# Scalar-tensor-tensor forms on VectorE and a later turn of the probabilities in a two-block transformer forward pass

## What is computed

```python
logits = jnp.einsum('bqhd,bkhd->bhqk', qf[:, q0:q1], kf[:, :q1]) * scale
bias = c[:, :, q0:q1, None] - c[:, :, None, :q1]
logits = jnp.where(mask[None, None], logits + bias, NEG)
p = jax.nn.softmax(logits, axis=-1)
outs.append(jnp.einsum('bhqk,bkhd->bqhd', p, vf[:, :q1]))
```

```python
acc = conv_b
for j in range(CONV_W):
    acc = acc + a_pad[:, j:j + L] * conv_w[j]
return jnp.einsum('blf,fd->bld', jax.nn.silu(acc) * b, w_down)
```

## Time and profile before

| | |
|---|---|
| median of three runs | 2684.56 us |
| the profiled execution | 2669.68 us, its span 2667.7 us |
| TensorE matmuls busy | 2459.9 us (92%), 12039 matmuls |
| GpSimd, ScalarE, VectorE busy | 1205.8, 897.2, 866.2 us |
| chain that ended last | TensorE 75%, GpSimd 9%, issue 8%, VectorE 4%, ScalarE 3% |
| granted TensorE clock, mean | 0.96 |

### The profile page before, as it was taken

The page is one execution under the profiler, slowest core; times in us unless marked ns, Lnnn a source line. Parts: engine busy times, 40 slices in busy tenths (PEclk is TensorE's granted clock), DMA queues, the critical chain, the costliest instruction groups (busy, mean ns, idle before and its releaser), DMA issues.

```text
span 2667.7 us, 31984 instructions
## 1 busy us (share of the span) xinstructions
PE 2459.9 (92%) x12039; PEld 1981.4 (74%) x12039; DVE 866.2 (32%) x1466; ACT 897.2 (34%) x1247; POOL 1205.8 (45%) x1032
## 2 busy tenths in 40 slices
PE   7898989979999989888888999998899989999997
PEld 6676757657888867766776888886688778889886
DVE  2434343441122131356543111222445322313222
ACT  3223232243322343344434332234432223323222
POOL 4353444434444446566553444444521234555552
PEclk8898989789999999999999999999999999999999
DMA  3211212112222212211112222321311111332331
GB/s 104 64 47 63 61 49 63 48 47 95 95 94 94 94 55 87 56 47 39 47 48 72 95 93 91 98 94 48 91 48 48 47 49 48 95 94 79 94 88 55
DMA packets 230943, 188.56 MB, mean 71 GB/s; under 512 B 8960, under 2 KB 222397, under 8 KB 230733
## 3 DMA queue, kind: packets, MB, share of 16 engines
q1 hardware_dynamic: 227152, 183.66, 22.4%
q10 hardware_dynamic: 3708, 3.79, 0.5%
HBM read 185.30 MB, written 2.10 MB: 70 GB/s over the span
## 4 chain that ended last, share of the span: by engine, by line
PE 75%; POOL 9%; issue 8%; DVE 4%; ACT 3%; DMA 0%; SPq 0%; POOLq 0%; DVEq 0%; ACTq 0%
PE ps L2232 54%; PE ps L1219 7%; POOL w_lo L1610 5%; PE ps L587 2%; PE ps L2263 1%; PE ps L2376 1%; PE ps L2354 1%; PE ps L1278 1%; PE ps L1189 1%; PE ps L1327 1%; POOL a_lo L1618 1%; PE ps L2379 1%; POOL xs L1665 1%; ACT w_hi L1737 1%; PE ps L1323 0%
## 5 line engine op out<-in xcount | busy, mean ns | idle before, releaser
L1610 POOL TENSOR_TENSOR w_lo<-raw,w_hi 128x512 fp32r<-128x512 f32 (+2 forms) x728 | 892.6, 1257 | 1013.6 <-ACT w_hi L1737 1013.4
L2232 PE MATMUL ps<-a_hi,w_hi 128*128 128x512 f32 (+1 forms) x1744 | 637.6, 382 | 61.7 <-POOL w_lo L1610 24.3
L2232 PE MATMUL ps<-a_lo,w_hi 128*128 128x512 f32 (+1 forms) x1744 | 629.7, 378 | 0.0
L2232 PE MATMUL ps<-a_hi,w_lo 128*128 128x512 f32 (+1 forms) x1744 | 629.7, 377 | 0.0
L1737 ACT ACTIVATE w_hi<-raw 128x2048 fp32r<-128x2048 f32 (+2 forms) x182 | 328.3, 1804 | 508.1 <-PE ps L2232 446.2
L2232 PEld LDWEIGHTS ps<-a_hi,w_hi 128*128 128x128 f32 x1744 | 323.0, 191 | 145.0 <-issue 64.9
L2232 PEld LDWEIGHTS ps<-a_hi,w_lo 128*128 128x128 f32 x1744 | 322.9, 192 | 62.2 <-issue 1.0
L2232 PEld LDWEIGHTS ps<-a_lo,w_hi 128*128 128x128 f32 x1744 | 322.1, 192 | 62.9
L2232 PE MATMUL ps<-b_hi,w_hi 128*128 128x512 f32 x912 | 360.2, 395 | 7.5 <-POOL b_lo L1678 4.3
L2232 PE MATMUL ps<-b_hi,w_lo 128*128 128x512 f32 x912 | 361.3, 396 | 0.0
L2232 PE MATMUL ps<-b_lo,w_hi 128*128 128x512 f32 x912 | 359.4, 394 | 0.0
(11 more groups left out here) (302 smaller groups left out, 2810.2 us busy)
## 6 DMA issues: line engine op xcount, KB each, us to landing
raw<-in_mlp_w_dram SPq DMA_DIRECT2D x128, 512.0 KB, 4.3
raw<-in_w_up_dram SPq DMA_DIRECT2D x44, 512.0 KB, 5.0
raw<-in_ssd_w_in_dram SPq DMA_DIRECT2D x32, 512.0 KB, 4.7
raw<-in_hgrn_w_in_dram SPq DMA_DIRECT2D x24, 512.0 KB, 4.6
raw<-in_w_in_dram SPq DMA_DIRECT2D x24, 512.0 KB, 4.9
raw<-in_ssd_w_out_dram SPq DMA_DIRECT2D x16, 512.0 KB, 4.5
raw<-in_ple_w_gate_dram SPq DMA_DIRECT2D x16, 512.0 KB, 4.0
raw<-in_w_down_dram SPq DMA_DIRECT2D x16, 512.0 KB, 4.0
```

Of the source, the lines that this page charges most:

```text
L1610: last = nc.gpsimd.tensor_tensor(w_lo[:, slot, piece], raw[:, slot, piece], w_hi[:, slot, piece].bitcast(F32), ALU.subtract)
L2232: last = nc.tensor.matmul(ps[:, b + s, 0:nn], w[:, k, m * P:(m + 1) * P], v[:, k, c0 + s * nn:c0 + (s + 1) * nn], start=(k == 0 and first) ...
```

## The change

All edits but two turn a VectorE instruction into a scalar_tensor_tensor that computes the same: `(in0 * 1.0) op in1` instead of `in0 op in1`. In L1042 a per-row scalar product becomes a product with the scalar and with a column of ones read with stride 0; in L1152 scale and bias by two per-row scalars becomes a scale by a scalar and a sum with the bias column read with stride 0. The low parts of the weights are made in four pieces in both kernels. In TensorE's attention steps with keys beyond the meta tokens (qb above 0) the fills are cut in two, with the values between, and the turn of the next step comes behind all of them.

```diff
@@ hgrn_dve, level
-  nc.vector.tensor_tensor(halves_of(hdd[:, i % 4], m, True), up, ref, ALU.subtract)
+  nc.vector.scalar_tensor_tensor(out=halves_of(hdd[:, i % 4], m, True), in0=up, scalar=1.0, in1=ref,
+                                 op0=ALU.mult, op1=ALU.subtract)
-  nc.vector.tensor_tensor(halves_of(hdd[:, i % 4], m, False), ref, low, ALU.subtract)
+  nc.vector.scalar_tensor_tensor(out=halves_of(hdd[:, i % 4], m, False), in0=ref, scalar=1.0, in1=low,
+                                 op0=ALU.mult, op1=ALU.subtract)
@@ hgrn_dve, end of a head; alike: roped (add), gated of retention (mult), summed (add),
@@ mlp_dve's b_lo (subtract), ple_dve's addition (add), the SSD groups' em by cbm (mult)
-  nc.vector.tensor_tensor(ho[:].unsqueeze(1), ho[:].unsqueeze(1), xc[:, bass.ds(h, 1), 0:T], ALU.mult)
+  nc.vector.scalar_tensor_tensor(out=ho[:].unsqueeze(1), in0=ho[:].unsqueeze(1), scalar=1.0,
+                                 in1=xc[:, bass.ds(h, 1), 0:T], op0=ALU.mult, op1=ALU.mult)
@@ block2_dve, normed
-  nc.vector.tensor_scalar(fp[0:q, n % 2, 0:nk], fp[0:q, n % 2, 0:nk], fm[0:q, n % 2, 3:4], None, ALU.mult)
+  nc.vector.scalar_tensor_tensor(out=fp[0:q, n % 2, 0:nk], in0=fp[0:q, n % 2, 0:nk],
+                                 scalar=fm[0:q, n % 2, 3:4], in1=ones[0:q, 0:1].broadcast_to([q, nk]),
+                                 op0=ALU.mult, op1=ALU.mult)
@@ block2_dve, ffn
-  own.did(nc.vector.tensor_scalar(acc[:], au[:, 4:516], taps[2], taps[3], ALU.mult, ALU.add))
+  own.did(nc.vector.scalar_tensor_tensor(out=acc[:], in0=au[:, 4:516], scalar=taps[2],
+                                         in1=taps[3].broadcast_to([P, T]), op0=ALU.mult, op1=ALU.add))
@@ block2_pe, the attention steps
-                fill(per_step[s] if n < N_FOX - 2 else 3)
+                half = per_step[s] // 2 if n < N_FOX - 2 else 1
+                if qb:
+                    fill(half)
+                    values(n)
+                    fill((per_step[s] if n < N_FOX - 2 else 3) - half)
+                else:
+                    fill(per_step[s] if n < N_FOX - 2 else 3)
                 if n + 1 < N_FOX:
                     turn_p(n + 1)
-                if qb:
-                    values(n)
```

More of the change, by code:

```diff
@@ L508, in level @@
                     ref = low[:, :, m - 1:m].broadcast_to([P, T // (2 * m), m])
-                    nc.vector.tensor_tensor(halves_of(hdd[:, i % 4], m, True), up, ref,
-                                            ALU.subtract).then_inc(dd_ready, 1)
+                    nc.vector.scalar_tensor_tensor(out=halves_of(hdd[:, i % 4], m, True), in0=up, scalar=1.0, in1=ref,
+                                                   op0=ALU.mult, op1=ALU.subtract).then_inc(dd_ready, 1)
                     if before:
                         dve.wait_ge(*before)
-                    nc.vector.tensor_tensor(halves_of(hdd[:, i % 4], m, False), ref, low,
-                                            ALU.subtract).then_inc(dd_ready, 1)
+                    nc.vector.scalar_tensor_tensor(out=halves_of(hdd[:, i % 4], m, False), in0=ref, scalar=1.0, in1=low,
+                                                   op0=ALU.mult, op1=ALU.subtract).then_inc(dd_ready, 1)
                 def scores(i):
@@ L552, in head @@
                 dve.wait_ge(on_ready, h * 2 + 1)
-                nc.vector.tensor_tensor(ho[:].unsqueeze(1), ho[:].unsqueeze(1), xc[:, bass.ds(h, 1), 0:T],
-                                        ALU.mult).then_inc(on_ready, 1)
+                nc.vector.scalar_tensor_tensor(out=ho[:].unsqueeze(1), in0=ho[:].unsqueeze(1), scalar=1.0,
+                                               in1=xc[:, bass.ds(h, 1), 0:T], op0=ALU.mult,
+                                               op1=ALU.mult).then_inc(on_ready, 1)
                 b_at.add()
@@ L1041, in normed @@
                 own.wait()
-                nc.vector.tensor_scalar(fp[0:q, n % 2, 0:nk], fp[0:q, n % 2, 0:nk], fm[0:q, n % 2, 3:4], None,
-                                        ALU.mult).then_inc(f_pn, 1)
+                nc.vector.scalar_tensor_tensor(out=fp[0:q, n % 2, 0:nk], in0=fp[0:q, n % 2, 0:nk],
+                                               scalar=fm[0:q, n % 2, 3:4], in1=ones[0:q, 0:1].broadcast_to([q, nk]),
+                                               op0=ALU.mult, op1=ALU.mult).then_inc(f_pn, 1)
             def by_sin(i, e):
@@ L1055, in roped @@
                     dve.wait_ge(r_sin, 2 * i + (e + 1))
-                    nc.vector.tensor_tensor(t, t, fv[e][:], ALU.add).then_inc(r_rope, 1)
+                    nc.vector.scalar_tensor_tensor(out=t, in0=t, scalar=1.0, in1=fv[e][:], op0=ALU.mult,
+                                                   op1=ALU.add).then_inc(r_rope, 1)
             def decayed(i, e, kb):
@@ L1081, in gated @@
                     dve.wait_ge(r_on, 2 * h + 1)
-                    nc.vector.tensor_tensor(ro[e][:], ro[e][:], gates[:, h, :], ALU.mult).then_inc(r_on, 1)
+                    nc.vector.scalar_tensor_tensor(out=ro[e][:], in0=ro[e][:], scalar=1.0, in1=gates[:, h, :],
+                                                   op0=ALU.mult, op1=ALU.mult).then_inc(r_on, 1)
                 b_at.add(2)
@@ L1974, in summed @@
                         own.wait()
-                    ins = nc.vector.tensor_tensor(lv[:, 0:T], res[:, 0, 0:T] if m == 1 else lv[:, 0:T], res[:, m, 0:T],
-                                                  ALU.add)
+                    ins = nc.vector.scalar_tensor_tensor(out=lv[:, 0:T], in0=res[:, 0, 0:T] if m == 1 else lv[:, 0:T],
+                                                         scalar=1.0, in1=res[:, m, 0:T], op0=ALU.mult, op1=ALU.add)
                     if m < KD - 1:
@@ L2018, in mlp_dve @@
                         dve.wait_ge(bhi_ready, b_at(1))
-                        nc.vector.tensor_tensor(b_lo[:, k, 0:T], hv[:, k % 4], b_hi[:, k, 0:T].bitcast(F32),
-                                                ALU.subtract).then_inc(blo_ready, 1)
+                        nc.vector.scalar_tensor_tensor(out=b_lo[:, k, 0:T], in0=hv[:, k % 4], scalar=1.0,
+                                                       in1=b_hi[:, k, 0:T].bitcast(F32), op0=ALU.mult,
+                                                       op1=ALU.subtract).then_inc(blo_ready, 1)
                         b_at.add()
@@ L2038, in ple_dve @@
                         dve.wait_ge(free_dve, fd(-1 if m < KD else 0))
-                        nc.vector.tensor_tensor(xc[:, m - 1, 0:T], xc[:, m - 1, 0:T], res[:, m - 1, 0:T],
-                                                ALU.add).then_inc(xc_ready, 1)
+                        nc.vector.scalar_tensor_tensor(out=xc[:, m - 1, 0:T], in0=xc[:, m - 1, 0:T], scalar=1.0,
+                                                       in1=res[:, m - 1, 0:T], op0=ALU.mult,
+                                                       op1=ALU.add).then_inc(xc_ready, 1)
                 pub.add(KD)
@@ L2148, in group @@
                     dve.wait_ge(em_ready, g * 8 + (r + 1))
-                    nc.vector.tensor_tensor(em[r % 3], em[r % 3], cbm[:].rearrange("p c l -> p (c l)"),
-                                            ALU.mult).then_inc(m_ready, 1)
+                    nc.vector.scalar_tensor_tensor(out=em[r % 3], in0=em[r % 3], scalar=1.0,
+                                                   in1=cbm[:].rearrange("p c l -> p (c l)"), op0=ALU.mult,
+                                                   op1=ALU.mult).then_inc(m_ready, 1)
                     if r + 2 < HPG:
```

## The result

The changed kernel takes 2694.52 us (median of 20 runs, 2683.02 to 2704.09) and the kernel before, run beside it, 2685.64 (20 runs, 2676.18 to 2691.91): a ratio of 1.0034, with an interval of 1.0020 to 1.0048, or +8.9 us. The forecast was +6 and 2690.5. The sum was nearly right, and the trace shows that it was right for a reason only partly the forecast one.

A forecast was written before the change was run, and what follows sets the result against it. TensorE was taken to bound the attention steps wholly. The terms 0 + 0 + 0 + 5.9 = +6 us made 2669.7 into 2675.6 on the profiled execution, 2690.5 us on the median, with a range of 2674 to 2703.

The forecast's parts named there:

- What bounds the kernel: TensorE bounds the attention steps wholly, busy 154.23 of 155.00 us; edits elsewhere pay only where TensorE waits.
- Part 1: VectorE's tensor_tensor turned into scalar_tensor_tensor with a constant scalar: taken as 0, between -0.7 and +3.5 us.
- 0.5 us a head: Sign against the forecast: an HGRN head shorter or longer by over 0.5 us.
- the faster rival: Forms free GpSimd or shorten VectorE's waits, shrinking HGRN and weight waits: -13 us, 2671; chance 0.15.
- Part 2: First tap of the gated MLP (L1152) loses its fast form: +0.27 us each, covered, cost 0.
- Part 3: Normalisation of attention probabilities (L1042) loses its fast form: 5.6 us of VectorE, cost 0 to +2 us, taken 0.
- Part 4: TensorE's new attention order: values stall for copies out of PSUM in seven steps, 5.9 us in sum.
- a slice 0.78: In attention, the fill slice between logits and values takes 0.78 us, counted towards the values' arrival at 1968.7.
- Sum: Whole kernel: 0 + 0 + 0 + 5.9 = +6 us, 2675.6 on the profiled execution, 2690.5 on the median.
- the stalls reach further: In attention, longer normalisation delays turn, copies and values in a chain: +16 us, 2700; chance 0.20.
- Halved throughput: New forms take +0.53 us per 512 columns in HGRN, mask products, norms and MLP: +48, 2732; chance 0.05.
- nothing: Attention order changes nothing, since ScalarE takes the copy before the weight chunk: 2684.6; chance 0.05.

The follow-up runs named there:

- e1: All scalar_tensor_tensor forms of the change, with TensorE's order as in the kernel before; 2687.05 us, ratio 1.0009.
- e2: TensorE's new order alone, with the VectorE forms of the kernel before; 2695.52 us, ratio 1.0039.
- e3: Kernel before, but a step's values come behind its whole fill and ahead of the next step's turn; 2684.1 us, ratio 0.9995.
- e5: Kernel before, but in 23 of 40 attention steps the previous step's values stand behind the first fill slice; 2702.46 us, ratio 1.0063.
- e6: Kernel before, but in 26 of 40 attention steps the logits stand behind the first fill slice; 2685.99 us, ratio 1.0019.
- e8: Change's order with the forms of before, but in steps s = 0, 3 and 6 values stand behind the whole fill; 2686.75 us, ratio 1.0017.
- e12: Kernel before, with the change's order in steps s = 3 to 7 alone (16 of 32 steps cut); 2689.0 us, one run.
- a tidy experiment: Change's order with the forms of before, but in steps s = 6 values come behind the whole fill; 2689.41 us, ratio 1.0013.
- e11: Kernel before, with the change's order in steps s = 6 and 7 alone (8 of 32 steps cut); 2688.05 us, ratio 0.9999.
- e13: The changed kernel profiled a second time, nothing altered; 2693.76 us, one run.

## Why the prediction was right, and where not

- **What bounds the kernel**: right. Only attention's length changed beyond the spread of executions; e1 and e2 show that the order alone makes the slowdown.
- **Part 1, constant-scalar forms at nothing**: right. 694 ns for 694, the level differences 418 for 418 (median), the product of decay and scores 684 for 684; the heads of HGRN begin 12.6 and end 13.6 us later than before, so all eight together are 1 us longer, under the 0.5 us a head that would have refuted it. GpSimd was not freed: the waits for the products of the levels are 24.0 us for 21.3, and that is no cost of the forms either, since they are 22.7 to 25.2 us in the runs with before's forms there (e2, e3, e5, e6, e8 to e12); the faster rival fell.
- **Part 2, first tap**: right in size and in cover. The last tile of a gated MLP round, after, with TensorE's wait for it; it answers to the earlier trace rows:

```profile
2369.65 1.09 DVE L1156 SCALAR_TENSOR_TENSOR acc<-au,pcol 128x512 f32<-128x512 f32 x1 [5.80 <-ACT au L938]
2370.89 1.56 DVE L1159 SCALAR_TENSOR_TENSOR acc<-au,pcol,acc 128x512 f32<-128x512 f32 x1
...
2374.52 0.69 DVE L1168 TENSOR_TENSOR hv<-acc,ps 128x512 f32<-128x512 f32 x1 [1.18 <-PE ps L2244]
```
```profile
PE ps L2244 <- DVE hv L1168: 3.0, 3, 1.0
```

  0.27 us longer (1.09 for 0.82), VectorE's idle time ahead of the product 0.27 shorter (1.18 for 1.45), TensorE's three waits unchanged.
- **Part 3, normalisation**: 0.77 us for 528 columns as worked out. Taken at 0 of 0 to 2: in before's order it costs two waits, 0.4 us, in the new order none.
- **Part 4, the new order**: the sum was right (5.9 forecast; 6.2 - 0.7 = 5.5 came), the list of waits was not. Behind n = 0, 13, 20 and 33 the wait for ScalarE's copy came as said, with 0.36, 0.70, 0.36 and 0.70 us for 0.8, 0.85, 0.8 and 0.85. Behind n = 6, 16 and 26, where 1.0, 0.6 and 1.0 stood, the values did not wait; the slice ahead of them did, 1.10, 1.02 and 1.10 us, for the bank under evacuation. Behind n = 36, where nothing stood, 0.3 us came by the same cause. The step that failed is "a slice 0.78", taken as work that can always start: I asked when the values' own inputs are ready, but not whether the slice that moves forward with them has its bank. The waits on ScalarE were put 1.2 us too high (3.3 for 2.1), the others 0.9 too low (2.6 for 3.5); that these nearly cancel is luck.
- **What was costed at nothing**: cutting the run of fill matmuls. It costs 0.1 us a time in 32 steps, 3.3 us in all, and moving the values ahead of the turn some 0.2. This is the term that is missing in "Sum". With it the account against the second profile nearly closes, in hundredths: 164.03 - 153.37 = 10.66 us = 5.56 waits + 3.32 first pairs + 0.25 place + 0.93 values of step 38 inside the stretch, and 0.60 not accounted for. Without the 0.93 the order costs 9.7 us in the trace, for 8.9 (whole change) and 10.6 (e2) in the timed medians.
- **The rivals**: the turn never waited for the normalisation in the changed kernel, against "the stalls reach further" (e5 shows that it can: seven such waits). Halved throughput and "nothing" fell as well. Of the 4 us above the forecast 1.1 are before's own median (2685.64 in 20 runs for the 2684.56 that was forecast from); the other 2.9 have the size of the cuts, with the half clock on top in some executions. The timed runs alone could not show that term: it is read from the traces.

## What to carry over

Whoever moves a piece of work past another on a saturated engine must ask two questions of every instruction that comes earlier by it: are its inputs ready, and is the place free that it writes. The work that stood in between may have hidden another engine's evacuation of that very bank. And an explanation that rests on one profile wants the same kernel profiled again before it is believed: one profile of the changed kernel differed from another by 3 us in the very stretch at issue, and a tidy experiment agreed with a reading that its mirror did not bear out. A total that comes out as expected shows little as well: e6 did, with waits that nobody expected and a cut that cost a third of what was thought.

## What the runs showed of the hardware beyond that

- A run of 264-column matmuls that is interrupted by other matmuls pays 0.1 us in the first pair behind them (0.35 us for 0.24), with no wait in the trace, behind values (64-column weights, 128 columns) and behind logits alike; logits behind values pay it as well (0.44 us for 0.34 behind a fill, 400 columns). Why was not tried.
- The granted clock in attention fell to its lower level for 3.4 us at a time, and up to 10 us in e5, in four of fourteen profiles, each time within 2 us of the end of a wait of TensorE of 1.1 us or more for the evacuation; but three profiles with the same waits (e11, e12, e13) held 1.00. What decides between them, the chip among it, stays open.
- A product with per-row scalars over SBUF was cheaper as tensor_scalar than as scalar_tensor_tensor (0.82 for 1.09 us at 512 columns in the first tap, GpSimd's hold included in both), although the second input is a single column read with stride 0.
